# First units computed block by block beside the first modulation vectors and the filter pieces; shorter norm steps and unit pairs by block

## What is computed

```
s_lat, s_ctx = silu(c), silu(c_ctx)
sh1, sc1, g1, sh2, sc2, g2 = split(s_lat @ w_mod[l] + b_mod[l], 6)
xn = rmsnorm(h, norm1_g[l]) * (1 + sc1) + sh1
proj = xn @ w_in[l]
# hyena_filter, from the layer's small weights alone:
h = (hid @ w3).reshape(L, 2, HY_WIDTH) * exp(-t * abs(decay))
l1 = sum(abs(h_fwd)) + sum(abs(h_bwd[1:]))
filt = concatenate([h_fwd, 0, h_bwd[::-1]]) / l1
y = x0 * (long_conv(zv, filt) + zv * hy_bias)
h = h + g2 * squared_relu_mlp(rmsnorm(h, norm2_g[l]) * (1 + sc2) + sh2)
```

## Time and profile before

| | us |
|---|---|
| median of 3 runs | 1498.87 |
| lowest, highest | 1497.33, 1503.57 |
| the profiled execution | 1501.06 |
| its span, first to last instruction | 1499.3 |
| TensorE matmuls busy in it | 1396.3 (93%) |
| DVE, ACT, POOL busy | 785.0, 527.4, 218.3 |

### The profile page before, as it was taken

The page is one execution under the profiler, slowest core; times in us unless marked ns, Lnnn a source line. Parts: engine busy times, 40 slices in busy tenths (PEclk is TensorE's granted clock), DMA queues, the critical chain, the costliest instruction groups (busy, mean ns, idle before and its releaser), DMA issues.

```text
span 1499.3 us, 19479 instructions
## 1 busy us (share of the span) xinstructions
PE 1396.3 (93%) x8034; PEld 1122.9 (75%) x8034; DVE 785.0 (52%) x1090; ACT 527.4 (35%) x803; POOL 218.3 (15%) x203
## 2 busy tenths in 40 slices
PE   2799999999999999799999999979999899899996
PEld 0365775777777787477777777757869889799996
DVE  3475657333553564644333443346775566775664
ACT  3242346132222231333212332123464443464551
POOL 4300100150201134100000000220004202500012
PEclk8699999999999999899999999998999999999998
DMA  8422320444542124344534444422315564455552
GB/s 326 166 87 82 99 70 1 172 173 169 198 160 70 42 99 169 111 141 142 181 140 162 150 153 169 148 91 84 127 57 169 163 232 130 152 175 197 191 197 71
DMA packets 56584, 210.52 MB, mean 140 GB/s; under 512 B 6213, under 2 KB 7365, under 8 KB 55600
## 3 DMA queue, kind: packets, MB, share of 16 engines
q1 hardware_dynamic: 54176, 194.22, 37.5%
q0 software_dynamic: 2320, 15.05, 2.6%
HBM read 205.58 MB, written 3.67 MB: 140 GB/s over the span
## 4 chain that ended last, share of the span: by engine, by line
PE 86%; DVE 6%; ACT 2%; DMA 2%; POOL 1%; issue 1%; SPq 0%; DVEq 0%; ACTq 0%; POOLq 0%
PE ps L1227 25%; PE ps L1228 24%; PE ps L1229 24%; PE ps L1256 3%; PE ps L1435 2%; DVE normed L868 2%; PE ps L1530 1%; PE ps L1540 1%; DMA raw<-in_units 1%; PE ps L1446 1%; PE ps L1459 1%; DVE wl L816 1%; DVE rstd L861 1%; DVE xl L877 1%; PE ps L1327 1%
## 5 line engine op out<-in xcount | busy, mean ns | idle before, releaser
L1227 PE MATMUL ps<-xh,wh 128*128 128x512 f32 (+2 forms) x1376 | 475.5, 346 | 33.0 <-DVE xl L877 28.5
L816 DVE TENSOR_TENSOR wl<-raw,wh 128x1024 fp32r<-128x1024 f32 x272 | 359.5, 1324 | 250.0 <-ACT wh L592 246.8
L1228 PE MATMUL ps<-xl,wh 128*128 128x512 f32 (+2 forms) x1376 | 467.3, 340 | 0.0
L1229 PE MATMUL ps<-xh,wl 128*128 128x512 f32 (+2 forms) x1376 | 466.4, 339 | 0.0
L592 ACT ACTIVATE wh<-raw 128x1024 fp32r<-128x1024 f32 x272 | 286.9, 1055 | 319.5 <-PE ps L1229 315.9
L1227 PEld LDWEIGHTS ps<-xh,wh 128*128 128x128 f32 (+1 forms) x1376 | 261.6, 190 | 80.0 <-issue 39.9
L1229 PEld LDWEIGHTS ps<-xh,wl 128*128 128x128 f32 (+1 forms) x1376 | 261.7, 190 | 30.4
L1228 PEld LDWEIGHTS ps<-xl,wh 128*128 128x128 f32 (+1 forms) x1376 | 261.8, 190 | 29.0 <-issue 1.0
L1227 PE MATMUL ps<-hid_h,wh 128*128 128x512 f32 (+1 forms) x512 | 172.0, 336 | 0.0
L1228 PE MATMUL ps<-hid_l,wh 128*128 128x512 f32 (+1 forms) x512 | 170.6, 333 | 0.0
L1229 PE MATMUL ps<-hid_h,wl 128*128 128x512 f32 (+1 forms) x512 | 170.3, 333 | 0.0
(11 more groups left out here) (203 smaller groups left out, 1443.7 us busy)
## 6 DMA issues: line engine op xcount, KB each, us to landing
raw<-in_units SPq DMA_DIRECT2D x272, 512.0 KB, 3.3
mod_ring<-in_mod_units SPq DMA_DIRECT2D x80, 512.0 KB, 4.0
first_ring<-in_mod_units SPq DMA_DIRECT2D x16, 512.0 KB, 9.5
filters<-filt POOLq DMA_DIRECT2D x2, 1280.0 KB, 6.2
filt<-filters POOLq DMA_DIRECT2D x2, 1280.0 KB, 10.2
ftab<-in_fwd POOLq DMA_DIRECT2D x3, 768.0 KB, 5.1
h<-in_x POOLq DMA_DIRECT2D x1, 2048.0 KB, 18.6
counts<-in_counts POOLq DMA_DIRECT2D x2, 1024.0 KB, 5.2
```

The lines of the kernel that those rows point to most:

```text
L816: dve.tensor_tensor(wl[:, g % SLOTS, :], raw[:, g % SLOTS, :], wh[:, g % SLOTS, :].bitcast(F), ALU.subtract)\
L1227: pe.matmul(dst, w_h, m_h, start=first, stop=False)
L1228: pe.matmul(dst, w_h, m_l, start=False, stop=False)
L1229: return pe.matmul(dst, w_l, m_h, start=False, stop=last)
```

## The change

- **Pairs.** The sixteen first modulation units become eight pairs of 1 MB: pair m holds the columns of shift and scale of channel block m alone (`pair`, `turn_pair`, `copy_pair`, `add_pair`). Four slots, three of them in memory that the norm and filters use later.
- **Wave.** The first four units (q's three and kv's first) are done side by side in four banks: `wave_step(m)` issues their 12 matmuls of block m as soon as block m of x is ready. Between the steps lie the next pair and one piece of the taps (`filter_taps(i)`, eight pieces in all). The same form with two units follows the later norms (`wave` at ff1a of both layers and at q of layer 1).
- **Norm.** DVE multiplies by rstd (512 columns in one instruction) and takes the rest (one instruction); ACT scales and shifts in two halves (`norm_full`) and rounds (`norm_hi`). POOL does nothing of a norm any more, except the last.
- **Squares.** ACT squares the eight blocks of h, POOL and DVE add two pairs each, TensorE sums them in four matmuls. h comes in four pieces at the head of SP's queue.
- **Filters.** The even and odd parts are made by POOL, the spectra are copied undivided by ACT and stored one by one, filter 0's before filter 1's sums; the division moves into the mixing of the Hyena branch as a factor for each channel. The sums of absolutes are four matmuls of one column.
- **Widths.** The units of kpe, uq and pool_w are loaded and split at 256, 768 and 512 columns instead of 1024.

```diff
...
+UNIT_WIDTHS = {PHASES[layer, name].g0 + j: n for layer in range(DEPTH) for name, n in (("kpe", KB * ROPE), ("uq", 2 * QL), ("pool_w", 512))
+               for j in range(PHASES[layer, name].mains)}
...
+            for c in range(4):
+                sp.dma_start(h[:, 2 * c:2 * c + 2, :], x_in[:, 2 * c:2 * c + 2, :]).then_inc(h_in_s[c], 16)
...
+                    n = unit_width(i)
+                    sp.dma_start(raw[:, i % SLOTS, 0:n], units_in[i, :, 0:n]).then_inc(unit_loaded[i % SLOTS], 16)
+                elif kind == "pair":
+                    if i >= PAIR_SLOTS:
+                        sp.wait_ge(pair_done, i - PAIR_SLOTS + 1)
+                    sp.dma_start(pair_slots[i % PAIR_SLOTS], pairs_in[i]).then_inc(pair_loaded[i % PAIR_SLOTS], 16)
...
+                    else:
+                        sp.wait_ge(f_spec, 5 * DEPTH)
...
+            pool.wait_ge(h_in_s[3], 16)
             pool.dma_start(f_w3[:, :], f_w3_in).then_inc(f_w3_in_s, 16)
...
-            pool.dma_start(h[:, :, :], x_in).then_inc(h_in_s, 16)
+            for c in range(2):
+                pool.wait_ge(x_squared, 2 * c + 2)
+                pool.tensor_tensor(normed[:, 2 * c, :], normed[:, 2 * c, :], normed[:, 2 * c + 1, :], ALU.add).then_inc(x_paired_pool, 1)
+            pool.wait_ge(pair_loaded[1], 16)
+            pool.dma_start(ftab0[:, :, :], fwd_in).then_inc(ftab_in_s, 16)
...
+            def filter_parts(f):
+                for tb in range(2):
+                    pool.wait_ge(f_weighted, 4 * f + 2 * tb + 2)
+                    if f:
+                        pool.wait_ge(pair_done, KB)
+                    e = envelope[:, f, tb, :]
+                    pool.tensor_tensor(f_even[f][:, tb, :], e[:, 0:HY], e[:, HY:], ALU.add).then_inc(f_parts, 1)
+                    pool.tensor_tensor(f_odd[f][:, tb, :], e[:, 0:HY], e[:, HY:], ALU.subtract).then_inc(f_parts, 1)
...
+            def filter_save(f):
+                for i in range(5):
+                    pool.wait_ge(f_copied, 5 * f + i + 1)
+                    pool.dma_start(filt_scratch[f, :, i * HY:(i + 1) * HY], filt0[:, i * HY:(i + 1) * HY]).then_inc(f_saved[f][i], 16)
...
+            def norm_full(v, m):
...
-                    last = act.activation(xh_of[v // 2][:, m, t], normed[:, m, t], ACT.Identity, bias=mods[:, shift, m, s:s + 1])
-                last.then_inc(x_hi, 1)
+                    last = act.activation(normed[:, m, t], normed[:, m, t], ACT.Identity, bias=mods[:, shift, m, s:s + 1],
+                                          scale=scales[:, v, m, s:s + 1])
+                last.then_inc(x_full, 1)
+            def norm_hi(v, m):
+                act.wait_ge(x_full, KB * v + m + 1)
+                n = NORM_T[v]
+                act.activation(xh_of[v // 2][:, m, 0:n], normed[:, m, 0:n], ACT.Copy).then_inc(x_hi, 1)
...
+            def filter_copy(f, i):
+                if f:
+                    act.wait_ge(f_saved[0][i], 16)
+                act.wait_ge(f_spec, 5 * f + i + 1)
+                act.activation(filt0[:, i * HY:(i + 1) * HY], ps[:, 7 - (5 * f + i) % 2, :], ACT.Copy).then_inc(f_copied, 1)
...
+                first_square(m)
             filter_sines(0)
-            filter_sines(1)
...
+            std(0)
+            for g in range(2):
                 split(g)
-            for v in range(MOD_FIRST // KB):
-                copy_mod(v)
+            copy_pair(0)
+            for g in range(2, WAVE):
+                split(g)
+            for m in range(KB):
+                norm_full(0, m)
+                norm_hi(0, m)
+                if m + 1 < KB:
+                    copy_pair(m + 1)
+                if m == 0:
+                    filter_sines(1)
+                elif m == 1:
+                    filter_envelope(0)
+                elif m == 4:
+                    filter_envelope(1)
...
+            def norm_by_rstd(v, m):
+                n = NORM_T[v]
+                dve.tensor_tensor(normed[:, m, 0:n], h[:, m, 0:n], rstd[:, 0:n], ALU.mult).then_inc(normed_dve, 1)
+            def norm_lo(v, m):
+                n = NORM_T[v]
+                dve.wait_ge(x_hi, KB * v + m + 1)
+                dve.tensor_tensor(xl_of[v // 2][:, m, 0:n], normed[:, m, 0:n], xh_of[v // 2][:, m, 0:n].bitcast(F), ALU.subtract).then_inc(x_split, 1)
...
+            def filter_weighted(i):
+                f, tb, d = i // 4, i // 2 % 2, i % 2
...
+                e = envelope[:, f, tb, d * HY:(d + 1) * HY]
+                src = ps[:, 7 - i % 2, :]
+                if d:
+                    dve.scalar_tensor_tensor(e, src, not_first[:, tb:tb + 1], e, ALU.mult, ALU.mult).then_inc(f_weighted, 1)
+                else:
+                    dve.tensor_tensor(e, src, e, ALU.mult).then_inc(f_weighted, 1)
...
+            def add_pair(m):
+                dve.wait_ge(pair_turned, m + 1)
...
+                dve.tensor_tensor(mods[:, 0:2, m, :], turned, b_mod[:, 0:2, m, :], ALU.add).then_inc(pair_added, 1)
+                dve.wait_ge(pair_added, m + 1)
+                dve.scalar_tensor_tensor(scales[:, 0, m, :], mods[:, 1, m, :], 1.0, gains[:, 0, m, :], ALU.add, ALU.mult)\
+                   .then_inc(pair_ready, 1)
...
             filter_sine_argument(0)
-            filter_sine_argument(1)
-            for g in range(AHEAD):
...
+            for c in range(2, 4):
+                dve.wait_ge(x_squared, 2 * c + 2)
+                dve.tensor_tensor(normed[:, 2 * c, :], normed[:, 2 * c, :], normed[:, 2 * c + 1, :], ALU.add).then_inc(x_paired_dve, 1)
+            norm_rstd(0)
+            norm_by_rstd(0, 0)
...
+            for m in range(KB):
+                if m + 1 < KB:
+                    norm_by_rstd(0, m + 1)
+                norm_lo(0, m)
+                if m + 1 < KB:
+                    add_pair(m + 1)
+                if m == 0:
+                    filter_sine_argument(1)
+                elif m >= 2:
+                    filter_weighted(m - 2)
+            for i in (6, 7):
+                filter_weighted(i)
...
+            def pair(m):
...
+                for r in range(2):
+                    for j in range(4):
+                        mm = pe.matmul(ps[32 * j:32 * j + 32, 4 + m % 2, 0:256], silu_wide[:, 4 * r + j, :],
+                                       pair_slots[m % PAIR_SLOTS][:, 4 * r + j, :], start=r == 0, stop=r == 1)
+                mm.then_inc(pair_done, 1)
...
+            def wave_step(layer, k, units, n, ready):
+                pe.wait_ge(ready[0], ready[1] + k + 1)
+                for g, bank in units:
+                    if k == 0:
+                        pe.wait_ge(lo_ready, g + 1)
+                    mm = three(ps[:, bank, 0:n], *cols(g % SLOTS, 128 * k), xh_of[layer][:, k, 0:n], xl_of[layer][:, k, 0:n], k == 0, k == KB - 1)
+                    if k == KB - 1:
+                        mm.then_inc(unit_done, 1)
...
+            def wave(layer, units, n, ready):
+                for k in range(KB):
+                    wave_step(layer, k, units, n, ready)
...
+                if i == 0:
+                    pe.wait_ge(f_parts, 4 * f + 4)
+                if o >= 2:
+                    pe.wait_ge(f_copied, o - 1)
+                for tb in range(2):
+                    mm = pe.matmul(ps[:, 7 - o % 2, :], ftab0[:, tb, at:at + 128], part[:, tb, :], start=tb == 0, stop=tb == 1)
+                mm.then_inc(f_spec, 1)
...
-            for i in range(MOD_FIRST - 4, MOD_FIRST):
-                mod_unit(i)
-            turn_mod(1)
+            pair(0)
+            turn_pair(0)
+            pair(1)
+            first = [(g, WAVE_BANKS[g]) for g in range(WAVE)]
+            for m in range(KB):
+                if m + 1 < KB:
+                    turn_pair(m + 1)
+                wave_step(0, m, first, T, (x_split, 0))
+                if m + 2 < KB:
+                    pair(m + 2)
+                if m == 2:
+                    pe.wait_ge(f_w3_in_s, 16)
+                    pe.wait_ge(f_sin, 2)
+                if m >= 2:
+                    filter_taps(m - 2)
+            for i in (6, 7):
+                filter_taps(i)
...
-            pe.wait_ge(f_parts[0], 4)
-            pe.wait_ge(std_ready, 1)
-            filter_spectra(0)
-            pe.wait_ge(f_scaled[0], 2)
+            pe.wait_ge(f_weighted, 2 * 4)
+            for i in range(3):
+                filter_spectrum(0, i)
+            first_kv()
+            filter_spectrum(0, 3)
+            key_pe(0)
+            filter_spectrum(0, 4)
+            filter_l1(0)
+            for i in range(5):
...
+                    if half == "a":
+                        p = PHASES[layer, "ff1a"]
+                        wave(layer, [(p.g0 + j, act_bank(p, j)) for j in range(2)], n, (x_split, KB * (2 * layer + 1)))
+                        mod_events(p, 0)
+                        mod_events(p, 1)
```

530 lines of the change are left out of this document (292 added, 238 removed).

## The result

| | before | changed |
|---|---|---|
| median of 15 runs each, us | 1499.42 | 1491.26 |
| lowest, highest | 1495.22, 1506.26 | 1487.14, 1499.65 |
| ratio, 95% interval | | 0.9947 (0.9929 to 0.9966) |
| span of the profiled execution | 1499.3 | 1490.0 |
| TensorE busy in it | 1396.3 | 1395.6 |

The change brings 8 us, 0.5%. The forecast was 1477, a gain of 22; 1491.26 lies at the upper edge of its range (1463 to 1491). Of the two parts of that gain one came and one didn't. A table of marks shows which. Each mark is one and the same instruction in both kernels, and the last column is what the changed kernel has gained up to it.

A forecast was written before the change was run, and what follows sets the result against it. TensorE, busy 93% of the span, was taken as the bound, with waits in the head and later norms to remove. 1499.3 - 14.1 (head) - 8.1 (norms) = 1477.1 us of span, forecast 1477, range 1463 to 1491.

The forecast's parts named there:

- The first unit at 30: Head: first unit matmul starts at 30 us instead of 80.96, bounds 27 (sums early) and 33 (POOL's adds in DVE's way).
- A stall of 1.8 us in each step: Blocks, from block 2 on: TensorE idles 1.8 us per step while DVE weights the tap piece before multiplication and rest.
- POOL beside DVE, 1.7 at each of two blocks: Blocks 4 and 6: POOL's even and odd parts slow DVE's multiplication and rest, 1.7 us each, 3.4 together.
- Blocks 2 to 5 at 2.4 GHz: Wave steps of blocks 2 to 5: TensorE at the higher clock, 6.8 us each, 27.2 in all.
- rivals 1 and 2: TensorE at 1.2 GHz through the blocks (1500 us, chance 0.14), or on into the spectra too (1510, chance 0.06).
- the forecast's 96 us: Head, from first unit matmul at 30 to gate_c0 at 126.4: forecast as 96.4 us.
- The tail of 41.8: From the end of the blocks (84.6) to gate_c0 (126.4): taps, spectra, kv and kpe units, sums, 41.8 us.
- From gate_c0 on "the same": Behind the head: work from gate_c0's first matmul on is the same in both kernels.
- The norms 3.4, 4.4 and 0.3: Three later norms: gains of 3.4 us (layer 0 ff1a), 4.4 (layer 1 q), 0.3 (layer 1 ff1a), together 8.1.
- (a): Layer 0, ff1a norm: TensorE starts at 612.8 instead of 615.08, both units done at 625.8 instead of 629.96; gain 3.4 us.
- (b): Layer 1, q norm: first matmul at 1010.6 instead of 1012.87, ACT's blocks rule, clock stays 0.50; gain 4.4 us.
- Small edits nothing: Narrow splits and the mixing's added factor, beside TensorE's gate units: no effect, bounds 0 and 1.2 us.

The follow-up runs named there:

- experiment 1: Changed kernel with four unused float32 matmuls filling TensorE's stall ahead of each block from block 3 on: 1484.77 us, ratio 0.9891.
- experiment 8: The changed kernel profiled once more, nothing altered: 1486.76 us.
- experiment 5: Changed kernel with the two units at the three later norms done one after the other instead of in pairs: 1499.11 us, ratio to before 0.9994.
- experiment 9: Changed kernel with all units loaded and split at 1024 columns again, as before the change: 1502.17 us in one execution.

## Why the prediction was wrong

- **The first unit at 30**: 32.07, inside the bounds 27 to 33. What was off here is "TensorE's four sums then end at about 18": 21.2. DVE's two additions took 4.05 us instead of 1.4 beside POOL's two, which the upper bound had named, but they were done at 16.9. From 16.5 on TensorE's passes started 0.85 us apart, twice the 0.43 of the spectra: they ran at the lower level, which nothing had named. Behind them 1.1 us came back.
- **A stall of 1.8 us in each step**: right in place and cause, 1.51, 2.58, 1.45, 2.57, 1.45. The dear ones are blocks 4 and 6 with POOL beside.
- **POOL beside DVE, 1.7 at each of two blocks**: 1.1 each (0.68 to 1.75), 2.1 together against 3.4. Too high there, but the same cause was not looked for where it cost most, at the split of unit 4: 4.12 us instead of 1.22. The prediction had listed these splits as lying beside the spectra. In two other executions the same split took 1.6. The Trainium skill, page "SBUF — State Buffer", section "Who interferes with whom", names who issues first as what decides who is blocked. The traces agree that either side can be the one that waits. POOL's operations follow one another without a gap in both executions. In the one with 4.12 POOL's own operation that starts beside the split takes 1.34; in the one with 1.59 it takes 2.26. Why DVE was held over more than one of POOL's operations in the first is open.
- **Blocks 2 to 5 at 2.4 GHz**, and the same for what follows them: this is the step that failed. The clock is 0.50 in parts of blocks 3, 4, 6 and 7, and after it at the kv unit and at gate_c0. In the blocks this costs some 8 us (an estimate: half of TensorE's busy time in these falls), at the other two places 1.7 each. The blocks were 5.5 us longer than forecast and not 8, since the other terms of the blocks together were forecast some 2.5 too dear. The prediction knew two rows, 0.50 with TensorE busy on modulation units and taps and 1.00 after 4 us of dense unit matmuls, and put the steps with their 1.8 us of idleness on the dense side, with rivals 1 and 2 (1.2 GHz throughout, 1500, and on into the spectra, 1510) as the alternatives. What happened lies between: up and down, up to six falls, and not in the same places from one execution to the next. Filled stalls (experiment 1) gave the forecast's 96 us back (53.2 for the blocks where 54.6 were forecast, 42.8 behind them where 41.8 were), so the sum's other terms hold to 1.4 us. The Trainium skill, page "TensorE: Matmul & The Clock Gate", section "Part 1: The HAM clock gate (the "warmup" mystery)", says that activity releases the throttle and that the phase differs from run to run. The traces agree: with one code of the head the falls lie in blocks 3, 4, 6 and 7 in this profile, in 2, 3, 4, 6 and 7 in experiment 8 and in 4, 6 and 7 in experiment 5, and gate_c0 starts at 139.2, 134.9 and 132.8.
- **The tail of 41.8**: 47.0. The wait for the kv unit (13.6 us from the end of the blocks instead of 10.2) is 3.4 of the 5.2 missing, and half of the low-clock stretch from 105.8 to 109.4 the rest. Spectra (8.69) and latent sums (4.56 + 1.69) are as in the earlier trace rows.
- **From gate_c0 on "the same"**: not its first 4 us, which ran at 0.50 (140 to 143), 1.6 us. It is no fixed price of the change: from gate_c0 to the first gate activation it is 7.4 us in seven of the thirteen profiled executions and 5.8 in six (the kernel before among them), though the wait ahead is 0.35 in all thirteen. What decides it is open.
- **The norms 3.4, 4.4 and 0.3**: 3.35, 4.2 and 0.3. In (a) the first matmul came 4.3 us behind the reciprocal (3.9 forecast). In (b) the clock was to stay at 0.50 until past 1022; it rose 5.8 us behind the first block's start with six matmuls a block (13.1 with three, experiment 5), and ACT's pace of 1.5 us a block then ruled all the same.
- **Small edits nothing**: near enough. The narrow split of pool_w does shorten a wait of TensorE by 0.7 to 1.3 us, which was not looked for, but TensorE comes to that wait later, and the start behind it is 0.4 us earlier in this execution (experiment 9).

As a sum: 22 forecast; head 14.1 - 2.1 (start) - 5.5 (blocks) - 5.2 (tail) - 1.6 (behind gate_c0) = -0.3; norms 7.9; pool_w and the clock behind it 1.6; together 9.2 of span. All of these are of one execution each side, and the clock's part of them (5.5, 1.6, 1.6) changes with the execution.

## What to carry to other kernels

A stall of 2 us in a row of short bursts cost more than 2 us here: in the changed kernel's profile TensorE's clock fell in four of the five bursts behind such a stall. Such gaps are to be taken away first, by order (here three lines on DVE, 18 us), and a step's time is not to be added up at 2.4 GHz while it holds them. Whatever stands ahead of an operation on which the next burst waits belongs behind it if its own reader can wait a step. And an engine taken out of the critical path can still slow another: POOL's additions made DVE's subtractions beside them 1.75 us long instead of 0.68, and once 4.12 instead of 1.22. Place its work where DVE has slack, and look at several executions before a few us of one head are believed.
